# A delta-rule inverse packed as two diagonal blocks of 64, each block on its own quarter of TensorE

## The chip, the cores and the metric

The kernel runs on one core of one Trainium2 chip. The metric is the time of one execution on the device in microseconds (us). TensorE (PE) multiplies matrices, VectorE (DVE) and ScalarE (ACT) do elementwise work, SyncE (SP) issues the weight transfers. The four run from separate instruction streams and meet at semaphores.

## The reference, cut to what matters

Two model blocks run one after the other on 512 tokens. The first has two layers, and each of them holds a gated delta rule with 4 heads of 128. In each chunk of tokens the rule solves a unit lower triangular system:

```
a = jnp.where(strict, jnp.einsum('bhnik,bhnjk->bhnij', k_beta, k) * rel, 0.0)
eye = jnp.broadcast_to(jnp.eye(C, dtype=jnp.float32), a.shape)
rhs = jnp.concatenate([v * beta[..., None], k_beta * jnp.exp(decay)[..., None]], axis=-1)
sol = lax.linalg.triangular_solve(eye + a, rhs, left_side=True, lower=True, unit_diagonal=True)
```

The kernel uses chunks of 128 tokens, so it needs the inverse of `eye + a` for 4 chunks x 4 heads in each of the 2 layers. All of it is in fp32.

## The kernel before, in words

`gdn_pe`, `gdn_act` and `gdn_dve` hold the delta rule of one layer, one function for each engine's own stream. The four chunks are n = 0 to 3 (`TT` = 4). A tile 128x512 holds the four heads (`GH` = 4) of one chunk side by side, 128 columns each. `at_mat` is the transposed matrix a. `xt_inv` is the transposed inverse X^T as it grows, and `x_inv` is X.

The inverse is built by doubling. At level 0 the 2x2 diagonal blocks are inverted, by a mask (`level0`) and a subtraction from the identity. For each later level s (1 to 6) the blocks of size 2^s are joined in pairs:

1. DVE masks `at_mat` to the blocks of that level, into `tmp` (L1727, in `level`).
2. PE multiplies that by X (`level`, L1430), ACT copies the product out of PSUM into `yv` (L1596).
3. PE multiplies the product into X^T (`update`, L1443), DVE subtracts the result from X^T (L1754).
4. PE turns the new X^T into X by a transposing matmul (`turn`, L1417), ACT copies it out (L1586, in `turned`).

Level 6 joins the two blocks of 64. It uses only the corners that matter, with 64x64 matmuls (L1427, L1440), ACT copies of 64x256 (L1594) and DVE subtractions of 64x256 (L1754 in its short form). The turn before it is a 64x64 one as well (L1414, L1584).

The order on every engine is written out by hand. PE does the four updates of a level with the turns of the earlier chunks between them, then the four products of the next level with the last turn behind the first of them. PE waits in program order. PSUM has 8 banks that `claim` hands out in turn, and a bank is claimed again only when its reader has freed it.

Ahead of the levels stands a stretch in which the four chunks' rows, grams and scaled copies are made (L737, L1392, L1396, L1401 on PE, L1572, L1578, L1559 and L1563 on ACT, L1703 and L1712 on DVE). The first turns and the level-1 products are mixed into it. DVE's work of one chunk there is `products`: `at_mat` (L1712), `level0` (L1718), the first mask (L1727) and the subtraction from the identity (L1722). Behind the levels comes the recurrence over the chunks. It begins with L1489, which waits for the finished X^T, and pieces of the output projection (L648 to L650) are mixed in.

Between the levels DVE also does two 128x512 products of the attention matrix and the queries (`queries`, L1738 and L1741), at the start of levels 2 to 5. ACT applies Silu to one gate tile (`gate_act`, L1189) behind levels 1 to 4.

Every fp32 matmul shows in the trace as two records of a weight load and a matmul. A transposing one shows as one record of each. Other lines that the prediction uses: L832 and L868 are scores and values of the attention stages, where two heads of 64 take either two halves of the array's rows (L832, each head with a PSUM bank of its own) or two halves of its columns (L868, both heads in one bank). L591 to L593 are the big weight products.

Of the kernel before, what the change touches and what calls it, by code (L numbers as in the profile page):

```python
# [13 lines left out]
P = 128  # L14
D = 1024
KC = D // P
S = 512
# [184 lines left out]
def const_columns():  # L202
    c = Columns()
    for name in ("ident", "ones", "upto", "neg_future", "rope1", "rope2", "head_ones"):
        c.add(name, P)
    for s in range(7):
        c.add(f"level{s}", P)
    c.add("inv_freq", 1)
    c.add("eps", 1)
    c.add("eps_q", 1)  # L210
    c.add("zero", 1)
    return c


def constants():
# [25 lines left out]
    for s in range(7):  # L241
        put(f"level{s}", ((i >> s) % 2 == 1) & ((j >> s) == (i >> s) - 1))
# [122 lines left out]
def build(nc, dram, out, book):  # L365
# [18 lines left out]
    with ctx:  # L384
# [27 lines left out]
        with ExitStack() as a2:  # L412
            x_inv = sb(a2, "x_inv", [P, TT, S])
# [934 lines left out]
        UPPER, LOWER = slice(0, HALF), slice(HALF, P)  # L1348

# [57 lines left out]
        def gdn_pe(pe, l):  # L1407

            def turn(s, n):
                pe.wait_ge(*when("xt", l, s, n))  # L1410
                b = claim(pe, "xtr", l, s, n)
                for h in range(GH):
                    if s == 5:
                        mm = pe.transpose(head(b, h)[UPPER, 0:HALF], head(xt_inv[:, n, :], h)[UPPER, 0:HALF],  # L1414
                                          ident[UPPER, 0:HALF])
                    else:
                        mm = pe.transpose(head(b, h), head(xt_inv[:, n, :], h), ident)  # L1417
                mm.then_inc(*filled("xtr", l, s, n))

            def level(s, n):  # L1420
                if s < 6:
                    pe.wait_ge(*when("level", l, s, n))
                pe.wait_ge(*when("x", l, s - 1, n))
                b = claim(pe, "y", l, s, n)
                for h in range(GH):
                    if s == 6:
                        mm = pe.matmul(head(b, h)[LOWER, 0:HALF], head(at_mat[:, n, :], h)[UPPER, HALF:P],  # L1427
                                       head(x_inv[:, n, :], h)[UPPER, 0:HALF], start=True, stop=True)
                    else:
                        mm = pe.matmul(head(b, h), head(tmp[:, 4 + n, :], h), head(x_inv[:, n, :], h),  # L1430
                                       start=True, stop=True)
                mm.then_inc(*filled("y", l, s, n))

            def update(s, n):
                pe.wait_ge(*when("y_in", l, s, n))
                b = claim(pe, "pxt", l, s, n)
                for h in range(GH):
                    y = head(yv[:, n, :], h)
                    if s == 6:
                        mm = pe.matmul(b[UPPER, HALF * h:HALF * h + HALF], y[LOWER, 0:HALF],  # L1440
                                       head(xt_inv[:, n, :], h)[LOWER, HALF:P], start=True, stop=True)
                    else:
                        mm = pe.matmul(head(b, h), y, head(xt_inv[:, n, :], h), start=True, stop=True)  # L1443
                mm.then_inc(*filled("pxt", l, s, n))

            for n in range(1, TT):
                gdn_rows_pe(pe, l, n)
                gdn_grams_pe(pe, l, n)
                if n >= 2:
                    turn(0, n - 2)  # L1450
                if n >= 3:
                    level(1, n - 3)
            for n in range(TT - 2, TT):
                turn(0, n)
# [110 lines left out]
        def gdn_act(act, l):  # L1565
# [15 lines left out]
            def turned(s, n):  # L1581
                b = bank(act, "xtr", l, s, n)
                if s == 5:
                    op = act.activation(corner(x_inv[:, n, :], UPPER, 0), corner(b[:, :], UPPER, 0), ACT.Copy)  # L1584
                else:
                    op = act.activation(x_inv[:, n, :], b[:, :], ACT.Copy)  # L1586
                op.then_inc(*freed("xtr", l, s, n, also=("x", l, s, n)))

            def level(s, n):
# [5 lines left out]
                else:  # L1595
                    op = act.activation(yv[:, n, :], b[:, :], ACT.Copy)  # L1596
                op.then_inc(*freed("y", l, s, n, also=("y_in", l, s, n)))

            for n in range(TT):
                products(n)  # L1600
                scaled("kt", k_dec, KD, "kdec", n)
                if n >= 2:
                    turned(0, n - 2)
# [7 lines left out]
            for n in range(TT - 2, TT):  # L1611
                turned(0, n)
                level(1, n - 1)
            level(1, TT - 1)
            for s in range(1, 6):
                for n in range(1, TT):
                    turned(s, n - 1)
                level(s + 1, 0)
                turned(s, TT - 1)
                for n in range(1, TT):  # L1620
# [76 lines left out]
        def gdn_dve(dve, l):  # L1697
# [10 lines left out]
            def products(n):  # L1708
# [8 lines left out]
                xt3 = xt_inv[:, n, :].rearrange("p (h n) -> p h n", h=GH)  # L1717
                dve.tensor_tensor(xt3, at_mat[:, n, :].rearrange("p (h n) -> p h n", h=GH),  # L1718
# [1582 lines left out]
```

## Time and profile before

| what | value |
|---|---|
| median of 3 executions | 2566.98 us (2565.72 to 2568.05) |
| profiled execution, its own time | 2569.73 us |
| span of the profiled execution, first to last instruction | 2567.9 us |
| mean granted TensorE clock | 0.991 of full |
| PE busy | 2487.4 us, 97% of the span |
| DVE busy | 1655.4 us, 64% |
| ACT busy | 1126.9 us, 44% |
| levels 1 to 5 of the inverse in layer 0, up to level 6's first update | 229.52 to 272.87 us |
| the same in layer 1 | 1115.03 to 1158.40 us |

Times in the profile count from the span's start. A row of a timeline gives the start, the length up to the last end in the row, the engine, the line and the number of instructions joined in it. The length of a row holds the tail of its last instruction, so the pace of a stream is read from one row's start to the next row's start.

### The profile page before, as it was taken

Reading aid. Unit: us, or ns where it says so; the run is one execution under the profiler, and the core shown is the slowest. Engines: PE = TensorE matmul, PEld = TensorE weight load, DVE = VectorE, ACT = ScalarE, POOL = GpSimd, SP = SyncE. Lnnn points to the kernel's source line nnn. Section 1 sums busy time; section 2 is a strip of 40 time slices with the busy share of each in tenths; the row PEclk is TensorE's granted clock in tenths of the full one; section 3 lists DMA queues with packets and bytes.
Section 4 is the critical chain, followed back from the end, with each engine's and each line's share of the span. In section 5 each row is a group of like instructions: output and inputs, shape, how many; then the busy total and the mean of one; then the engine's idle time right before and its main releaser. Section 6 shows DMA issues by size and latency. Waiting matters only on the chain.

```text
span 2567.9 us, 34478 instructions
## 1 busy us (share of the span) xinstructions
PE 2487.4 (97%) x13166; PEld 2012.4 (78%) x13166; DVE 1655.4 (64%) x3170; ACT 1126.9 (44%) x2089; POOL 0.2 (0%) x4
## 2 busy tenths in 40 slices
PE   8998999999999999999999999999999999999998
PEld 6878888778888778798977888887866666788666
DVE  6666575464447785665744644488586677599774
ACT  4336454443333243464544423333446667232573
POOL 0000000000000000000000000000000000000000
PEclk9999999999999999999999999999999999999999
DMA  4220043222237522201422232464110000132311
GB/s 166 90 74 17 27 139 99 65 83 93 96 99 237 164 83 86 75 1 50 157 65 75 82 97 93 145 223 160 58 42 18 17 17 21 62 89 66 87 48 50
DMA packets 74083, 219.37 MB, mean 85 GB/s; under 512 B 21312, under 2 KB 21568, under 8 KB 73152
## 3 DMA queue, kind: packets, MB, share of 16 engines
q1 hardware_dynamic: 48384, 176.29, 21.0%
q10 hardware_dynamic: 25536, 40.87, 5.1%
q8 instruction: 107, 1.75, 0.3%
q14 instruction: 56, 0.46, 0.1%
HBM read 215.03 MB, written 2.10 MB: 85 GB/s over the span
## 4 chain that ended last, share of the span: by engine, by line
PE 87%; DVE 7%; ACT 3%; issue 2%; ACTq 0%; DMA 0%; DVEq 0%
PE bank L591 21%; PE bank L592 20%; PE bank L593 20%; PE bank L832 4%; PE bank L868 4%; PE bank L842 3%; DVE w_lo L553 2%; PE bank L1443 1%; PE bank L1430 1%; PE bank L622 1%; PE bank L624 1%; PE bank L623 1%; ACT w_hi L546 1%; PE bank L648 1%; PE bank L650 1%
## 5 line engine op out<-in xcount | busy, mean ns | idle before, releaser
L546 ACT ACTIVATE w_hi<-w_raw 128x1024 fp32r<-128x1024 f32 x334 | 354.3, 1062 | 572.4 <-PE bank L593 523.5
L553 DVE TENSOR_TENSOR w_lo<-w_raw,w_hi 128x1024 fp32r<-128x1024 f32 x334 | 408.1, 1223 | 234.8 <-ACT w_hi L546 233.8
L591 PE MATMUL bank<-a_hi,w_hi 128*128 128x512 f32 x1344 | 539.3, 401 | 20.0 <-DVE w_lo L553 18.0
L593 PE MATMUL bank<-a_hi,w_lo 128*128 128x512 f32 x1344 | 525.7, 391 | 0.0
L592 PE MATMUL bank<-a_lo,w_hi 128*128 128x512 f32 x1344 | 525.2, 391 | 0.0
L591 PEld LDWEIGHTS bank<-a_hi,w_hi 128*128 128x128 f32 x1344 | 251.9, 187 | 82.6 <-issue 18.4
L593 PEld LDWEIGHTS bank<-a_hi,w_lo 128*128 128x128 f32 x1344 | 251.8, 187 | 55.6
L592 PEld LDWEIGHTS bank<-a_lo,w_hi 128*128 128x128 f32 x1344 | 252.3, 188 | 52.5 <-issue 1.0
L591 PE MATMUL bank<-b_hi,w_hi 128*128 128x512 f32 x440 | 182.9, 416 | 4.2 <-DVE w_lo L553 2.7
L592 PE MATMUL bank<-b_lo,w_hi 128*128 128x512 f32 x440 | 173.2, 394 | 0.0
L593 PE MATMUL bank<-b_hi,w_lo 128*128 128x512 f32 x440 | 172.8, 393 | 0.0
L591 PE MATMUL bank<-f_hi,w_hi 128*128 128x512 f32 x352 | 137.0, 389 | 0.0
L593 PE MATMUL bank<-f_hi,w_lo 128*128 128x512 f32 x352 | 136.9, 389 | 0.0
L592 PE MATMUL bank<-f_lo,w_hi 128*128 128x512 f32 x352 | 136.9, 389 | 0.0
L3025 DVE CUSTOM_DVE_ANT_0 mod_part<-mod_raw,mod_cond,par 128x1024 f32<-128x1024 f32 x96 | 118.6, 1281 | 0.0
L591 PEld LDWEIGHTS bank<-b_hi,w_hi 128*128 128x128 f32 x440 | 82.9, 188 | 35.1 <-issue 28.3
L2960 DVE TENSOR_TENSOR tmp<-bank,rstd 128x512 f32<-128x512 f32 x44 | 30.4, 690 | 112.1 <-PE bank L593 112.1
L593 PEld LDWEIGHTS bank<-b_hi,w_lo 128*128 128x128 f32 x440 | 82.9, 188 | 19.0
L2420 DVE SCALAR_TENSOR_TENSOR c_y<-c_u,par,c_y 128x512 f32<-128x512 f32 x120 | 90.2, 751 | 3.7
L591 PE MATMUL bank<-m_hi,w_hi 128*128 128x256 f32 (+1 forms) x296 | 88.8, 300 | 0.8 <-DVE w_lo L553 0.8
L592 PEld LDWEIGHTS bank<-b_lo,w_hi 128*128 128x128 f32 x440 | 83.3, 189 | 7.7 <-issue 1.0
L593 PE MATMUL bank<-m_hi,w_lo 128*128 128x256 f32 (+1 forms) x296 | 88.0, 297 | 0.0
(444 smaller groups left out, 4453.3 us busy)
## 6 DMA issues: line engine op xcount, KB each, us to landing
w_raw<-w_tiles SPq DMA_DIRECT2D x334, 512.0 KB, 3.5
mod_raw<-mod_tiles ACTq DMA_DIRECT2D x48, 512.0 KB, 4.2
d_bias<-rpb_rows ACTq DMA_DIRECT2D x16, 224.0 KB, 4.3
hT<-xT ACTq DMA_DIRECT2D x8, 256.0 KB, 6.0
m_in<-memT ACTq DMA_DIRECT2D x2, 1024.0 KB, 4.8
mod_cond<-cond_rows ACTq DMA_DIRECT2D x2, 1024.0 KB, 5.9
out<-hT ACTq DMA_DIRECT2D x8, 256.0 KB, 2.2
ctx_sq<-ctxT ACTq DMA_DIRECT2D x1, 1024.0 KB, 7.7
```

The source lines that it names most:

```text
L546: act.activation(w_hi[:, t % SPLIT, :], w_raw[:, t % RAW, :], ACT.Copy).then_inc(sem("w_rounded"), 1)
L553: dve.tensor_tensor(w_lo[:, t % SPLIT, :], w_raw[:, t % RAW, :], w_hi[:, t % SPLIT, :].bitcast(f32), ALU.subtract).then_inc(sem("w_split"), 1)
L591: pe.matmul(o, wh, chunk(hi, k, n), start=k == 0, stop=False)
L592: pe.matmul(o, wh, chunk(lo, k, n), start=False, stop=False)
L593: mm = pe.matmul(o, wl, chunk(hi, k, n), start=False, stop=k == kc - 1)
L622: pe.matmul(outs[j][:, :n], wh, hi[:, k, :n], start=k == 0, stop=False)
L832: mm = pe.matmul(b[:, :nk], q, k, start=j == 0, stop=j == len(mms) - 1)
L842: mm = pe.transpose(b[:, P * j:P * j + P], s[:, u % s.shape[1], c:c + P], ident)
L868: mm = pe.matmul(b[rows * lane:rows * lane + rows, lo - base:hi - base], v, pt(lane, kt, kt + 1, lo - base, hi - base)[:, 0, :], start=n = ...
L2420: op = dve.scalar_tensor_tensor(out=c_y[:, c, :], in0=c_u[:, c, j:j + S], scalar=G("dw_w", CT * c + j), in1=c_y[:, c, :], op0=ALU.mult, op ...
L2960: dve.tensor_tensor(tmp[:, r + 2, :], b[:, :], rstd[:, :], ALU.mult)\
L3025: dve.tensor_tensor_reduce(mod_part[:, w, :], mod_raw[:, c % MOD_RAW, :], mod_cond[:, w, :], 1.0, G(f"mod_b{l}", c), ALU.mult, ALU.add, mo ...
```

## The change

The inverses up to level 5 are kept as two diagonal blocks of 64, since nothing outside these blocks is touched before level 6. The upper block lies on partitions 0 to 63 and the lower one on partitions 64 to 127, so a chunk's four heads take 256 columns in place of 512. X and X^T then fit into one tile, `xx_inv`: X in columns 0 to 255, X^T in 256 to 511.

- Each 128x128 matmul of levels 1 to 5 becomes two of 64x64, one on the upper rows and columns of the array (first in `QUADS`) and one on the lower.
- The turns of levels 1 to 5 go. In their place `update` makes both products, the change of X and the change of X^T, and DVE subtracts both from `xx_inv` in one instruction.
- The turn after level 0 stays, as an ordinary matmul with `ident_half` in place of a transposing one.
- The masks are 64 wide. DVE copies the diagonal blocks of `at_mat` next to each other first (two copies of 64x256 for each chunk), and each mask product covers 128x256.
- DVE does the mask product of a level ahead of the subtraction instead of behind it.
- At level 5 DVE writes the new X^T into the corners of `xt_inv`, in two instructions, beside one for X. `xt_inv` gets a zero corner from four memsets, and level 6 writes its corner by a product with -1 in place of a subtraction.

```
+            def turn(n):
+                pe.wait_ge(*when("xt", l, 0, n))
+                b = claim(pe, "xtr", l, n)
                 for h in range(GH):
+                    for q in QUADS:
+                        mm = pe.matmul(half(b, 0, h)[q], half(xx_inv[:, n, :], 1, h)[q], C("ident_half")[q, :],
+                                       start=True, stop=True, skip_group_check=True)
...
             def level(s, n):
-                pe.wait_ge(*when("x", l, s - 1, n))
+                pe.wait_ge(*(when("x", l, n) if s == 1 else when("xt", l, s - 1, n)))
...
-                        mm = pe.matmul(head(b, h), head(tmp[:, 4 + n, :], h), head(x_inv[:, n, :], h),
-                                       start=True, stop=True)
+                        for q in QUADS:
+                            mm = pe.matmul(half(b, 0, h)[q], half(tmp[:, 4 + n, :], 0, h)[q],
+                                           half(xx_inv[:, n, :], 0, h)[q],
+                                           start=True, stop=True, skip_group_check=True)
...
             def update(s, n):
-                        mm = pe.matmul(head(b, h), y, head(xt_inv[:, n, :], h), start=True, stop=True)
+                        for q in QUADS[:1] if s == 5 else QUADS:
+                            pe.matmul(half(b, 0, h)[q], half(xx_inv[:, n, :], 1, h)[q], half(yv[:, n, :], 0, h)[q],
+                                      start=True, stop=True, skip_group_check=True)
+                        for q in QUADS:
+                            mm = pe.matmul(half(b, 1, h)[q], half(yv[:, n, :], 0, h)[q],
+                                           half(xx_inv[:, n, :], 1, h)[q],
+                                           start=True, stop=True, skip_group_check=True)
...
             for s in range(1, 7):
                 for n in range(TT):
                     update(s, n)
-                    if s < 6 and n:
-                        turn(s, n - 1)
                 if s < 6:
-                    level(s + 1, 0)
-                    turn(s, TT - 1)
-                    for n in range(1, TT):
+                    for n in range(TT):
                         level(s + 1, n)
...
+                for q, at in zip(QUADS, (0, HALF)):
+                    op = dve.tensor_copy(by_half(halves(tmp[q, 4 + n, :], 1)), corner(at_mat[:, n, :], q, at))
+                op.then_inc(*done("blocks", l, n))
+                dve.wait_ge(*when("blocks", l, n))
+                xt3 = by_half(halves(xx_inv[:, n, :], 1))
+                dve.tensor_tensor(xt3, blocks_of(n), over_halves(C("level0")), ALU.mult)\
+                   .then_inc(*done("level0", l, n))
...
+            for n in range(TT):
+                dve.memset(corner(xt_inv[:, n, :], LOWER, 0), 0.0)
...
                 for n in range(TT):
-                    b = bank(dve, "pxt", l, s, n)
-                        x, change = xt_inv[:, n, :], b[:, :]
-                    dve.tensor_tensor(x, x, change, ALU.subtract)\
                     if s < 5:
                         level(s + 1, n)
+                    b = bank(dve, "pxt", l, s, n)
+                    if s < 5:
+                        op = dve.tensor_tensor(xx_inv[:, n, :], xx_inv[:, n, :], b[:, :], ALU.subtract)
+                    elif s == 5:
+                        x = halves(xx_inv[UPPER, n, :], 0)
+                        dve.tensor_tensor(x, x, halves(b[UPPER, :], 0), ALU.subtract)
+                        for q, at in zip(QUADS, (0, HALF)):
+                            op = dve.tensor_tensor(corner(xt_inv[:, n, :], q, at),
+                                                   by_half(halves(xx_inv[q, n, :], 1)),
+                                                   by_half(halves(b[q, :], 1)), ALU.subtract)
```

## Rows read from the trace of the kernel before

**Rows 1.** The page: busy time, share of the span and count of each engine.

```profile
PE 2487.4 (97%) x13166; PEld 2012.4 (78%) x13166; DVE 1655.4 (64%) x3170; ACT 1126.9 (44%) x2089; POOL 0.2 (0%) x4
```

**Rows 2.** Stretches: start:end, length, busy (count) PE, PEld, DVE, ACT, POOL, clock, DMA.

```profile
229.52:238.52 9.00, 9.00 (x83) 8.93 (x82) 6.15 (x10) 4.61 (x8) 0.00 (x0) 1.00 0.01 2
...
265.52:272.87 7.35, 7.35 (x80) 6.56 (x78) 2.75 (x4) 3.46 (x9) 0.00 (x0) 1.00 0.01 2
...
1115.03:1158.40 43.37, 43.37 (x401) 42.27 (x400) 27.37 (x44) 24.94 (x44) 0.00 (x0) 1.00 0.01 1
...
1094.00:1115.14 21.14, 17.40 (x112) 17.11 (x113) 14.64 (x39) 16.81 (x50) 0.00 (x0) 0.76 0.01 1
```

**Rows 3.** The chain that ended last, level 1 of layer 0: start, length, what.

```profile
232.12 0.89 PE bank L1443 x8
233.01 0.44 PE bank L1417 x4
...
234.78 0.89 PE bank L1430 x8
```

**Rows 4.** The timeline from 220 us: idle time and its releaser in brackets.

```profile
220.16 1.13 DVE L1703 SCALAR_TENSOR_TENSOR rel_t<-bank,col,con 128x128 f32<-128x128 f32 x4 [0.85 <-ACT dec L1559]
...
227.27 0.66 PE L1417 MATMUL bank<-con,xt_inv 128*128 128x128 f32 x4 [1.14 <-DVE xt_inv L1722]
...
227.96 0.60 ACT L1586 ACTIVATE x_inv<-bank 128x512 f32<-128x512 f32 x1 [0.52 <-PE bank L1417]
...
229.62 1.95 PE L1443 MATMUL bank<-xt_inv,yv 128*128 128x128 f32 x16
...
230.72 0.69 DVE L1754 TENSOR_TENSOR xt_inv<-xt_inv,bank 128x512 f32<-128x512 f32 x1 [3.51 <-PE bank L1443]
231.32 0.68 DVE L1727 TENSOR_TENSOR tmp<-at_mat,con 128x512 f32<-128x512 f32 x1
```

**Rows 5.** The timeline of PE in layer 1, ahead of the levels.

```profile
1095.77 1.97 PE L1401 MATMUL bank<-con,g_qkv 128*128 128x128 f32 x8 [2.94 <-DVE at_mat L1712]
```

**Rows 6.** The timeline of PE around level 6.

```profile
269.28 1.16 PE L1443 MATMUL bank<-xt_inv,yv 128*128 128x128 f32 x8
270.37 0.41 PE L1414 MATMUL bank<-con,xt_inv 64*64 64x64 f32 x4
270.71 0.68 PE L1427 MATMUL bank<-x_inv,at_mat 64*64 64x64 f32 x8
...
272.87 0.27 PE L1440 MATMUL bank<-xt_inv,yv 64*64 64x64 f32 x1
```

**Rows 7.** The timeline of all engines where level 6's update begins.

```profile
272.93 0.22 PE L1427 MATMUL bank<-x_inv,at_mat 64*64 64x64 f32 x1
...
272.98 0.22 PE L1440 MATMUL bank<-xt_inv,yv 64*64 64x64 f32 x1
...
273.04 0.22 PE L1427 MATMUL bank<-x_inv,at_mat 64*64 64x64 f32 x1
273.10 1.85 PE L1440 MATMUL bank<-xt_inv,yv 64*64 64x64 f32 x29
...
274.88 1.16 PE L1489 MATMUL bank<-v_beta,xt_inv 128*128 128x128 f32 x8
```

**Rows 8.** Groups of matmuls, shapes apart: count, busy us, mean ns, idle before.

```profile
L868 PE MATMUL bank<-e_pt,e_vt 128*64 128x256 f32 x384 | 46.7, 385 | 5.4 <-ACT e_pt L992 5.4
...
L832 PE MATMUL bank<-xk,xq 128*128 128x256 f32 x128 | 33.0, 381 | 1.3 <-DVE xq L2882 1.3
L868 PE MATMUL bank<-x_pt,xvt 128*128 128x512 f32 x64 | 28.8, 592 | 0.0
...
L832 PE MATMUL bank<-e_kd,e_q 64*128 64x512 f32 x64 | 21.3, 641 | 0.0
```

**Rows 9.** Groups by shape, 229 to 275 us, DVE and ACT.

```profile
L1754 DVE TENSOR_TENSOR xt_inv<-xt_inv,bank 64x256 f32<-64x256 f32 x4 | 1.7, 414 | 2.6 <-PE bank L1440 2.4
...
L1594 ACT ACTIVATE yv<-bank 64x256 f32<-64x256 f32 x4 | 1.5, 380 | 0.9 <-PE bank L1427 0.5 <-PE bank L1440 0.4
```

More of the change, by code:

```diff
@@ L205, in const_columns @@
         c.add(name, P)
-    for s in range(7):
-        c.add(f"level{s}", P)
+    c.add("ident_half", P // 2)
+    for s in range(6):
+        c.add(f"level{s}", P // 2)
     c.add("inv_freq", 1)
@@ L240, in constants @@
     put("head_ones", (j // 64) == (i // 64))
-    for s in range(7):
-        put(f"level{s}", ((i >> s) % 2 == 1) & ((j >> s) == (i >> s) - 1))
+    jh, ih = j % (P // 2), i[:, :P // 2]
+    put("ident_half", jh == ih)
+    for s in range(6):
+        put(f"level{s}", ((ih >> s) % 2 == 1) & ((jh >> s) == (ih >> s) - 1))
     freq = np.float32(500000.0) ** (-np.arange(0, 2 * ROPE_HALF, 2, dtype=np.float32) / (2 * ROPE_HALF))
@@ L1348, in build, with half, halves, by_half @@
         UPPER, LOWER = slice(0, HALF), slice(HALF, P)
+        QUADS = (UPPER, LOWER)
+        def half(ap, w, h):
+            return ap[:, (GH * w + h) * HALF:(GH * w + h) * HALF + HALF]
+        def halves(ap, w):
+            return ap[:, GH * HALF * w:GH * HALF * (w + 1)]
+        def by_half(ap):
+            return ap.rearrange("p (h n) -> p h n", h=GH)
+        def over_halves(ap):
+            return ap[:, None, :].broadcast_to([P, GH, HALF])
         def l2_sums_pe(pe, l):
@@ L1449, in gdn_pe @@
                 if n >= 2:
-                    turn(0, n - 2)
+                    turn(n - 2)
                 if n >= 3:
@@ L1453, in gdn_pe @@
             for n in range(TT - 2, TT):
-                turn(0, n)
+                turn(n)
                 level(1, n - 1)
@@ L1579, in scaled, with turned @@
                 op.then_inc(*freed(name, l, n, also=(event, l, n)))
[L1581 to L1587, printed above, removed]
+            def turned(n):
+                b = bank(act, "xtr", l, n)
+                act.activation(halves(xx_inv[:, n, :], 0), halves(b, 0), ACT.Copy)\
+                   .then_inc(*freed("xtr", l, n, also=("x", l, n)))
             def level(s, n):
@@ L1595, in level @@
                 else:
-                    op = act.activation(yv[:, n, :], b[:, :], ACT.Copy)
+                    op = act.activation(halves(yv[:, n, :], 0), halves(b, 0), ACT.Copy)
                 op.then_inc(*freed("y", l, s, n, also=("y_in", l, s, n)))
@@ L1602, in gdn_act @@
                 if n >= 2:
-                    turned(0, n - 2)
+                    turned(n - 2)
                 if n + 1 < TT:
@@ L1611, in gdn_act @@
             for n in range(TT - 2, TT):
-                turned(0, n)
+                turned(n)
                 level(1, n - 1)
@@ L1735, in gdn_dve @@
                     products(n - 1)
+            for n in range(TT):
+                dve.memset(corner(xt_inv[:, n, :], LOWER, 0), 0.0)
             def queries(n):
```

43 lines of the change are left out of this document (13 added, 30 removed).

## The prediction

> **What bounds the kernel now.** I read the page first. TensorE (PE) is busy for 2487.4 us, 97% of the span [rows 1], so work taken off PE counts if nothing takes its place. Then I asked for stretches around the delta rule. One level there, from the first update of level 1 to that of level 2, takes 9.00 us. PE is busy for all 9.00, DVE for 6.15, ACT for 4.61 [rows 2]; levels 2 to 4 read the same within 0.01. Level 5 with the products of level 6 takes 7.35. The reader should see that DVE and ACT have room and PE has none.
>
> The chain of waits shows the same by pieces: an update of one chunk is 8 records in 0.89 us, a turn 4 records in 0.44, a product 8 records in 0.89 [rows 3]. Four chunks give 4 x (0.89 + 0.44 + 0.89) = 8.88, and 0.12 is left for waits. Layer 1 has the same 43.37 us over its levels [rows 2] (layer 0: 4 x 9.00 + 7.35 = 43.35).
>
> **What a 64x64 record costs.** Level 6 has such matmuls already, one tile at a time. L1414, 4 records, goes from 270.37 to 270.71, with a change of tile shape at its front: 0.085 us each. L1440's last 29 records start at 273.10 and L1489, which follows, starts at 274.88: 1.78 / 29 = 0.061, with the drain [rows 6, 7]. Eight L1427 at 270.71 last 0.68, and a single such record 0.22 [rows 6, 7], so seven steps take 0.46: 0.066 with the first one's start-up. I take 0.058, which is the step inside the alternating rows below, and keep 0.061 for the range. A 128x128 record steps by 0.89 / 8 = 0.111.
>
> Now the count. Before, a chunk and level has 20 records. After, the product has 4 heads x 2 tiles x 2 = 16, the update 4 x 4 x 2 = 32, together 48. One after the other these would take 48 x 0.058 = 2.78 us, against 2.22 before. So all depends on whether the two tiles run at the same time.
>
> **What the trace shows of two tiles at once.** Three places.
> - Where level 6's update begins, L1427 (upper rows, lower columns) and L1440 (lower rows, upper columns) alternate: L1440 at 272.87, L1427 at 272.93, L1440 at 272.98, L1427 at 273.04, L1440 at 273.10 [rows 6, 7]. Each tile steps by 0.055 to 0.06 on its own and does not slow the other. L1440 stands behind all of L1427 in the program, so it even ran past it.
> - Two halves of the columns, same bank: L868 with 64 columns takes 46.7 / 384 = 0.122 us for 256 moving columns, a full-array record of that length 33.0 / 128 = 0.258 [rows 8].
> - Two halves of the rows, a bank each: L832 with 64 rows takes 21.3 / 64 = 0.333 for 512, a full one 28.8 / 64 = 0.450 [rows 8]. This includes tails of groups with one pair only; it is weaker, but the same sign.
>
> What no row shows is the exact case: diagonal tiles for a long time, both writing one bank in different partitions.
>
> **The sum, layer by layer.**
> 1. Levels 1 to 4. With both tiles at work a chunk costs 24 x 0.058 = 1.39 us, a level 5.57. I add 0.09 for waits as before: 5.66. Removed against added: 9.00 - 5.66 = 3.34 a level, 13.4 for four.
> 2. Is DVE then the bound? Its two instructions of a chunk started 0.60 apart at 512 columns [rows 4]. A 64x256 subtraction took 0.414 against 0.69 at 512 [rows 4, 9], so the new 128x256 mask costs about 0.60 - 0.27 = 0.33. A chunk is 0.93, four are 3.7, with the two attention products (1.2) 4.9: under 5.66. The tightest wait is for chunk 3. Its update ends 3.71 + 0.2 after the level's start, DVE is through at about 4.6 to 4.7, and PE wants it at 3.71 + 3 x 0.46 = 5.1. If DVE's instructions did not overlap (0.69 + 0.41 a chunk), the level would be 5.8: 0.15 x 8 = 1.2 us in all, kept for the range. The mask product now stands ahead of the subtraction; it waits only for the earlier product, done long before.
> 3. ACT: the turned copies (0.60) go, the rest shrink from 0.60 to 0.38 [rows 4, 9]. A product of chunk 0 is out 0.46 + 0.2 + 0.38 = 1.0 us after its start, and the update that needs it starts 1.9 after. The gates' Silu lies in the free time. Each level claims 8 banks in place of 12, so a bank comes round after a level, long freed.
> 4. Level 5. The update's upper tile has 16 records for a chunk: 0.93, four 3.71. DVE needs three 64-row instructions a chunk, 3 x 0.34 = 1.0, and starts 1.14 in, so it ends at 5.3. Level 6's product of chunk 3 waits for that and ends near 5.8, where level 6's update begins. Before: 7.35 [rows 2], with pauses, for each switch between 128 and 64 wide tiles lengthened an update from 0.89 to 1.09 [rows 3, 6]. Gain 1.5.
> 5. Level 6's update and what follows keep their shape; the product with -1 costs what the subtraction did (0.41). Nothing.
> 6. Ahead of level 1. DVE's work for a chunk loses three 512-wide instructions and gets five 256-wide ones and one more wait: 3 x 0.60 against 5 x 0.33 + 0.1, even. DVE waits there for ACT (0.85 at 220.16) [rows 4], and ACT's turned copy ahead of it shrinks by 0.22. At the end, turn 3 starts at 227.27, its copy takes 0.60 at 227.96, and the first update starts at 229.62 after two products of 0.89 [rows 4]. After: turn to 227.95, copy to 228.35, one product of 0.46 behind it, update at 228.85. Together 0.9. The four memsets lie in DVE's idle 3.51 us before its first subtraction [rows 4].
> 7. The rest of the kernel hangs on PE's progress, so it moves up as it is. The masks' load shrinks; no PE wait hangs on it.
>
> Sum: 13.4 + 1.5 + 0.9 = 15.8 a layer, 31.6 for two. The profiled execution took 2569.73 (span 2567.9, 1.8 around it), 2.7 above the median, so it would be 2538.1, and the median 2566.98 - 31.6 = 2535.4 us.
>
> **Rivals.**
> - **The tiles take turns** (slower). If two tiles that write one bank cannot run together, a chunk costs 2.78, a level 11.2, 2.2 more than now, 8.9 a layer over four levels; level 5 comes out even (4 x 24 x 0.058 + 1.9 = 7.4). 2567.0 + 17.8 = 2585. It decides from 0.093 us for a pair of records on (8.91 / 96). For it: no row has row halves in one bank. Against it: L868's column halves share one and run together, and the partitions here are as separate as those. Chance 0.12. A page speaks for this rival: the Trainium skill, "TensorEngine Tiling (Array Packing)", "Gotcha 1: PSUM Pressure", says that different row tiles cannot access the same PSUM bank at the same time. By that rule the time would be this rival's 2585; no run here shows it yet, since L832's row tiles had a bank each.
> - **Instructions come too slowly.** Twice the records must be issued in each microsecond as in any long stretch before. The 6-record stretch at 272.87 may have lived on a queue filled ahead. If a pair takes 0.087, half way between both cases, a level is 8.4 (gain 0.6), level 5 gains 0.8, the front 0.4: 3.6 a layer, 2560. Chance 0.14. The Trainium skill, the same page, "Instruction Overhead", has about 60 cycles for a matmul however few its columns and advises against tiling an already small dimension; two of them at 2.4 GHz would be 0.05, under the 0.058 used here.
> - **The clock falls to 1.2 GHz** (slower), since each tile pair fills half the array. The levels then cost twice 0.058 for a pair, as in the first rival: 2585 or a little above. For it: in layer 1 the mean granted clock ahead of the levels was 0.76, in a stretch where PE had sat idle for 2.94 us [rows 2, 5]. Against it: the stretch with level 6's single 64x64 tiles ran at 1.00 [rows 2], and PE will not be idle. Chance 0.06.
> - A shift of where the low clock falls ahead of the levels: layer 1 needed 19.3 us from its first gap (1095.77) to level 1 (1115.03). A second such stretch in layer 0, or none in layer 1, is worth about 2.5 us either way. It changes the range, not the case.
>
> **How the numbers follow.** Both tiles together: 0.68, 2535.4, own range 2529 to 2545 (the clock 2.5 either way, 0.061 for 0.058 costs 8 x 0.29 = 2.3, DVE 1.2, the front and level 5 worth 1 a layer more or less). To leave out no more than 2 in 10 the range must take in the second rival to 2562: 2528 to 2562. About what this kernel's times can tell from no change is 0.2%, 5.1 us. Faster: 0.68 and most of the 0.14, 0.80. The same: 0.04. Slower: 0.16, both slow rivals less a little.
>
> **What would show it.** A level 5.6 to 5.8 us long with PE busy throughout, 192 matmul records in it, rows of upper and lower tile in pairs; DVE's idle time before a subtraction small; no record of L1417. Wrong, if a level takes 8.4 or 11.2 us, if the clock reads 0.5 inside the levels, or if PE waits for `xx_inv` in each level: then DVE is the bound and item 2 failed. Level 5 is wrong if level 6's update starts later than 6.5 us after level 5's first.

## The result

The changed kernel took 2534.8 us (median of 4 runs, 2533.35 to 2537.24), the kernel before on the same chip 2566.8 (4 runs). The ratio is 0.9877, with a 95% interval of 0.9862 to 0.9892: faster by 32 us. The forecast was 2535.4. One execution of the kernel before, in the first series of the experiments below, took 10193.89 us for a reason that nothing here shows, and no ratio counts it.

The page of the changed kernel, against [rows 1]: TensorE has 1,152 records more and is busy for 35.5 us less.

```profile
PE 2451.9 (97%) x14318; PEld 1978.0 (78%) x14318; DVE 1650.8 (65%) x3210; ACT 1093.9 (43%) x2049; POOL 0.2 (0%) x4
```

Stretches of the changed kernel, in the columns of [rows 2]. The first two are level 1 and level 3 of layer 0; then come level 1 and level 2 of layer 1, and the last is from level 5's first update to the first product of the recurrence (here L1507, before L1489).

```profile
231.41:237.01 5.60, 5.60 (x199) 5.60 (x197) 4.43 (x9) 1.32 (x4) 0.00 (x0) 1.00 0.01 3
242.83:249.16 6.33, 5.98 (x198) 5.79 (x196) 5.34 (x12) 2.09 (x6) 0.00 (x0) 1.00 0.01 3
...
1100.69:1106.29 5.60, 5.60 (x199) 5.60 (x197) 4.43 (x9) 1.32 (x4) 0.00 (x0) 1.00 0.01 3
1106.29:1111.89 5.60, 5.60 (x199) 5.60 (x197) 5.03 (x11) 3.45 (x7) 0.00 (x0) 1.00 0.02 6
1123.09:1131.41 8.32, 7.63 (x168) 7.29 (x164) 6.12 (x16) 3.74 (x10) 0.00 (x0) 1.00 0.01 2
```

The reader is to see 5.60 where [rows 2] have 9.00, at a granted clock of 1.00, with PE busy for all of it. The 199 records are the level's 192 and some that overlap the edges. The second row is longer and not busy throughout; I come back to it.

How both tiles work side by side is seen in the timeline of PE where level 1 of layer 1 begins. L1460 is X's change, L1463 that of X^T:

```profile
1100.69 0.31 PE L1460 MATMUL bank<-yv,xx_inv 64*64 64x64 f32 x4
1100.81 0.31 PE L1463 MATMUL bank<-xx_inv,yv 64*64 64x64 f32 x4
1100.93 0.31 PE L1460 MATMUL bank<-yv,xx_inv 64*64 64x64 f32 x4
1101.04 0.31 PE L1463 MATMUL bank<-xx_inv,yv 64*64 64x64 f32 x4
```

Four records start every 0.117 us, two of the upper and two of the lower tile (by the order of the loops): a pair each 0.058. All of a chunk's update write one bank. 96 pairs x 0.058 = 5.6 us.

**Where the 32 us come from.** By the starts of the stretches in both traces:

| stretch | layer 0 before, after | layer 1 before, after |
|---|---|---|
| last gap of PE ahead of the levels to level 1's first update | 16.82, 15.67 | 19.37, 16.63 |
| levels 1 to 4 | 36.00, 23.63 | 36.01, 22.40 |
| level 5's first update to the recurrence's first product | 9.26, 8.26 | 9.25, 8.32 |
| gain | 1.2 + 12.4 + 1.0 | 2.7 + 13.6 + 0.9 |

That is 31.8 of the 33.7 us by which the spans differ (2567.9 and 2534.2). The other 1.9 lie outside, and the low stretches of the clock account for most of them. The changed kernel reached layer 0's last gap 2.9 later (215.74 against 212.80). Its first products stepped by 0.43 us until 15.65, those of the kernel before only until 12.70, and by 0.23 from there. So it worked 2.95 us longer at the slow step, which did there what takes 1.6 at the fast one: 1.4 lost. And it had a stretch at half clock from 50.1 to 53.5, where the kernel before had none, for another 1.6. What follows layer 1's levels was 4.7 us shorter: the work there is the same (7,182 records of PE in both), but the kernel before spent 27.2 us of it at half clock and the changed one 17.0. By the same steps the 10.2 us between them are worth 4.7, if PE is the bound throughout. These three prices are estimates.

Ahead of the levels layer 0 had no low clock in either kernel, and gained 1.15. So of layer 1's 2.7 some 1.6, most of it, is the clock: the kernel before had two stretches at half clock there, the changed one only one.

```profile
1095.00:1101.80 6.80, 6.03 (x29) 6.04 (x30) 5.05 (x15) 4.79 (x15) 0.00 (x0) 0.50 0.00 1
1108.65:1112.06 3.41, 3.41 (x19) 3.41 (x18) 3.38 (x9) 2.30 (x8) 0.00 (x0) 0.50 0.03 5
```

These are of the kernel before. Of the changed one, with 3.4 us at half clock from 1084.3 on:

```profile
1084.06:1087.70 3.64, 3.64 (x18) 3.64 (x19) 1.91 (x6) 2.70 (x10) 0.00 (x0) 0.53 0.02 5
```

### The profile page after: what moved, and what is told of

Same layout as the page of the kernel before. It is cut to its first block, busy times and chain, and to the rows that moved or that the text cites. A ratio compares the mean times of both kernels' runs of the same rounds, so it can differ in the third digit from the quotient of the medians.

```text
span 2534.2 us, 36742 instructions
## 1 busy us (share of the span) xinstructions
PE 2451.9 (97%) x14318; PEld 1978.0 (78%) x14318; DVE 1650.8 (65%) x3210; ACT 1093.9 (43%) x2049; POOL 0.2 (0%) x4
## 4 chain that ended last, share of the span: by engine, by line
PE 86%; DVE 8%; ACT 4%; issue 2%; ACTq 0%; DMA 0%; DVEq 0%
PE bank L594 21%; PE bank L595 20%; PE bank L596 20%; PE bank L835 4%; PE bank L871 4%; PE bank L845 3%; DVE w_lo L556 2%; PE bank L625 1%; PE bank L627 1%; PE bank L626 1%; ACT w_hi L549 1%; PE bank L651 1%; PE bank L653 1%; PE bank L652 1%; PE bank L1463 1%
## 5 line engine op out<-in xcount | busy, mean ns | idle before, releaser
L596 PEld LDWEIGHTS bank<-b_hi,w_lo 128*128 128x128 f32 x440 | 82.6, 188 | 18.9
L595 PE MATMUL bank<-m_lo,w_hi 128*128 128x256 f32 (+1 forms) x296 | 88.0, 297 | 0.0
```

The costliest lines, as they stand in the source:

```text
L595: pe.matmul(o, wh, chunk(lo, k, n), start=False, stop=False)
L596: mm = pe.matmul(o, wl, chunk(hi, k, n), start=False, stop=k == kc - 1)
```

## The experiments

Eight kernels ran: the first four beside one series of the kernel before (2568.3 us median), the next three beside another (2566.8), the last beside a third (2566.3). Times are medians.

### Order of the tiles

Is it the alternation of upper and lower tile that makes both work? Here a chunk's products of the upper tile are all issued before those of the lower tile, in the turn, the product and the update. The records are the same ones.

```diff
-                for h in range(GH):
-                    for q in QUADS:
+                for q in QUADS:
+                    for h in range(GH):
```

> The same matmuls on PE in another order: in each group of levels 0 to 5 all of the upper tile's records first, then all of the lower tile's (8 and 8 in a product, 16 and 16 in an update). Theory: the gain hangs on both tiles at work at once, and a tile holds only a few records ahead (three were seen), so the tiles overlap only at the ends of groups. A level of layer 1 (5.60 us in the changed kernel) becomes 8 to 10 us, the time some 2555 to 2575 us. Rival 1, it is the smaller tile or the missing turns that gain, not the overlap: a level stays at 5.6 and the time at 2535. Rival 2, no overlap at all unless records alternate: 4 x 48 x 0.058 = 11.1 us a level, 5.5 x 8 = 44 us, about 2580. If PE looks past more than eight records the level also stays near 5.6; then the rows tell it from rival 1, since upper and lower records still start together.

Measured: 2555.87 us, 0.9954 of before (0.994 to 0.9969). A level takes 8.33 us in both layers. One stretch, layer 1's level that starts at 1111.27, and the timeline of PE at its start:

```profile
1111.27:1119.60 8.33, 8.33 (x198) 8.33 (x195) 4.94 (x10) 1.24 (x4) 0.00 (x0) 1.00 0.01 2
```

```profile
1111.27 0.27 PE L1461 MATMUL bank<-yv,xx_inv 64*64 64x64 f32 x1
1111.32 0.22 PE L1446 MATMUL bank<-xx_inv,tmp 64*64 64x64 f32 x1
1111.38 0.22 PE L1461 MATMUL bank<-yv,xx_inv 64*64 64x64 f32 x1
1111.38 0.22 PE L1446 MATMUL bank<-xx_inv,tmp 64*64 64x64 f32 x1
...
1111.44 0.22 PE L1446 MATMUL bank<-xx_inv,tmp 64*64 64x64 f32 x1
```

The update's first upper record (L1461) starts ahead of the last three lower records of the product (L1446), as L1440 did ahead of three L1427 in the kernel before ([rows 7] have the first of these three and the last; I give the other under the account of the prediction). Behind these rows only the upper tile works (L1461 and L1464 are both its own), record by record at 0.058, until the lower tile's come. The numbers close: 192 records one by one are 11.14 us; a level has 16 changes from one tile to the other, each with three steps side by side, so 11.14 - 16 x 3 x 0.058 = 8.36 against 8.33. Counted in this level's trace, at each of the 16 changes exactly three steps have a second record beside them, and at no other. So the gain of the tiles hangs on the order of issue. The six records in alternation that the prediction rested on [rows 6, 7] were this look ahead of three, not yet proof of a steady state; the change has that state because it issues the tiles in turn.

### Packed, with the turns kept

The tiles without the other half of the change: X is again the turned X^T (a turn of 8 pairs of records a chunk and level, copied by ACT), in place of the 8 pairs of X's change.

```diff
-                pe.wait_ge(*(when("x", l, n) if s == 1 else when("xt", l, s - 1, n)))
+                pe.wait_ge(*when("x", l, s - 1, n))
...
-                        for q in QUADS[:1] if s == 5 else QUADS:
-                            pe.matmul(half(b, 0, h)[q], half(xx_inv[:, n, :], 1, h)[q], half(yv[:, n, :], 0, h)[q],
...
                     update(s, n)
+                    if s < 6 and n:
+                        turn(s, n - 1)
```

> Packed in blocks of 64 as in the changed kernel, but X comes from a turn at levels 1 to 5, as before: the update makes only the change of X transposed, an identity matmul turns it and ACT copies it out. PE has as many 64x64 records a level (16 + 16 + 16 for a chunk). Theory: the turnless update gives no PE time, it only takes away waits; a level is 5.6 to 6.1 us, the time 2535 to 2540. Rival: the turn's chain (DVE, PE, ACT, PE) no longer fits into a level this short, as each step covers less work: a level of 6.5 to 7.5, the time 2543 to 2552.

Measured: 2538.62 us, ratio 0.9885 (0.9868 to 0.9903). A level takes 5.87 us in layer 1. Level 2 of that layer as a stretch, and PE's timeline at its start (L1464 is X^T's change, L1435 the turn, which begins anew behind each update):

```profile
1106.93:1112.80 5.87, 5.81 (x199) 5.68 (x196) 4.14 (x10) 4.82 (x11) 0.00 (x0) 1.00 0.02 6
```

```profile
1106.93 1.10 PE L1464 MATMUL bank<-xx_inv,yv 64*64 64x64 f32 x32
1108.08 0.68 PE L1435 MATMUL bank<-con,xx_inv 64*64 64x64 f32 x16
```

The count of records is the same as without turns (14318 on both pages). The extra 0.27 us a level is a wait of some 0.3 between the two rows: the first turn stands behind DVE's subtraction. Over eight levels this is 2.2 us, and ACT is busy for 4.82 in place of the changed kernel's 3.45. The packing carries nearly all of the gain; what the turnless update adds, 3.8 us by the medians and 2 by the ratios, is about as large as this kernel's times can tell: the changed kernel itself gave 2534.8 in one series and 2538.1 in another, below. The 2.2 us are read from the traces.

### DVE's order

The changed kernel puts the mask product of the next level ahead of the subtraction; here it stands behind, as before.

```diff
-                    if s < 5:
-                        level(s + 1, n)
                     b = bank(dve, "pxt", l, s, n)
...
                     op.then_inc(*freed("pxt", l, s, n, also=("xt", l, s, n)))
+                    if s < 5:
+                        level(s + 1, n)
```

> Only DVE's order undone: the mask product of the next level stands behind the subtraction again. Theory: the order is worth nothing, since DVE has about half a microsecond to spare for chunk 3 and the mask fits in it; 5.60 us a level, time within 0.1% of the changed kernel (2533 to 2537). Rival: the mask of chunk 3 comes too late for its product, 0.1 to 0.33 us a level, 1 to 3 us in all.

Measured: 2536.15 us, ratio 0.9876 (0.9855 to 0.9898), levels of 5.60 us in both layers. No difference. DVE has the room: in the changed kernel's timeline of DVE at level 1 of layer 1 a chunk takes 0.93, as forecast, and a level has idle time at its start. Below, L1771 subtracts, L1745 masks.

```profile
1101.86 0.69 DVE L1771 TENSOR_TENSOR xx_inv<-xx_inv,bank 128x512 f32<-128x512 f32 x1 [1.28 <-PE bank L1463]
1102.46 0.42 DVE L1745 TENSOR_TENSOR tmp<-tmp,con 128x256 f32<-128x256 f32 x1
1102.80 0.68 DVE L1771 TENSOR_TENSOR xx_inv<-xx_inv,bank 128x512 f32<-128x512 f32 x1
```

### Level 6's product waits for X alone

At level 5 DVE has three instructions a chunk: X's upper block (L1774), then the two blocks of X^T (L1776, twice). Level 6's product reads X alone, but waits for the last of the three. Here it waits for the first.

```diff
-                pe.wait_ge(*(when("x", l, n) if s == 1 else when("xt", l, s - 1, n)))
+                pe.wait_ge(*(when("x", l, n) if s == 1 else when("x_last", l, n) if s == 6 else when("xt", l, s - 1, n)))
...
-                        dve.tensor_tensor(x, x, halves(b[UPPER, :], 0), ALU.subtract)
+                        dve.tensor_tensor(x, x, halves(b[UPPER, :], 0), ALU.subtract).then_inc(*done("x_last", l, n))
```

> One event more: at level 5 DVE says that X is ready behind its first instruction of a chunk, and level 6's product waits for that in place of all three. Theory: in the changed kernel level 5 lasts 8.32 us up to the first product of the recurrence, 0.5 more than forecast, because DVE needs 1.22 us for a chunk and each product waits for the last of its three instructions. Then this run shortens it by 0.4 to 0.8 us a layer, about 1 us in all (2533 to 2535, not to be told from the changed kernel by time, but by the profile). Rival: the update of level 6 waits for the last corner anyway and the stretch stays at 8.2 to 8.3.

Measured: 2534.03 us, ratio 0.9865 (0.9848 to 0.9882). From level 5's first update to the recurrence's first product it takes 7.55 us in layer 0 and 7.54 in layer 1. The changed kernel's timeline there shows what was removed; PE first, then DVE:

```profile
1127.90 0.68 PE L1442 MATMUL bank<-xx_inv,at_mat 64*64 64x64 f32 x8 [0.16 <-DVE xt_inv L1776]
1129.12 0.50 PE L1442 MATMUL bank<-xx_inv,at_mat 64*64 64x64 f32 x5 [0.54 <-DVE xt_inv L1776]
1129.40 0.27 PE L1456 MATMUL bank<-xt_inv,yv 64*64 64x64 f32 x1
```

```profile
1124.24 0.41 DVE L1774 TENSOR_TENSOR xx_inv<-xx_inv,bank 64x256 f32<-64x256 f32 x1 [0.89 <-PE bank L1463]
1124.58 0.84 DVE L1776 TENSOR_TENSOR xt_inv<-xx_inv,bank 64x256 f32<-64x256 f32 x2
1125.45 0.41 DVE L1774 TENSOR_TENSOR xx_inv<-xx_inv,bank 64x256 f32<-64x256 f32 x1
```

DVE needs 1.21 us a chunk (1124.24 to 1125.45) and PE stands for its last instruction twice. With X alone awaited, 8.32 becomes 7.54, for 0.8 a layer. The trace shows it in both layers; the time of 2534.0 against 2534.8 can't.

### Neither packed nor turned

The other half of the change by itself: matrices of 128x128 as before, but X's change is computed in the update and subtracted by DVE, and the turns of levels 1 to 5 go.

```diff
             def update(s, n):
                 pe.wait_ge(*when("y_in", l, s, n))
+                if s < 6:
+                    b2 = claim(pe, "px", l, s, n)
+                    for h in range(GH):
...
+                            mm = pe.matmul(head(b2, h), head(xt_inv[:, n, :], h), y, start=True, stop=True)
...
-                    if s < 6 and n:
-                        turn(s, n - 1)
```

> The kernel before (matrices of 128x128) with the turns taken away and nothing packed: the update of levels 1 to 5 computes X's change as well as that of X^T, and DVE subtracts both, so a chunk has 24 products of 128x128 as before (8 for the level product, 8 for X's change, 8 for X^T's). My theory: what pays in the change is the packing; records of 128x128 step every 0.111 us with or without turns. Before, a level had 24 of them a chunk too, but 8 were turns that came in between; 4 x 24 x 0.111 = 10.7 us bounds a level where before took 9.00 (turns of 0.056 us a step). So a level gets longer by 1.7 us, 4 levels and 2 layers 13 us, level 5 about nothing: 2580 us, ratio 1.005. Rival: before was bound by its chain of turn and copy, and the turnless update alone carries a good part of the gain: a level below 9.0 us, and a time of 2550 or less.

Measured: 2585.73 us, ratio 1.0073 (1.0056 to 1.0089): slower. A level takes 10.72 in both layers, and from level 5 to the recurrence 10.47:

```profile
1134.45:1145.17 10.72, 10.72 (x99) 10.72 (x98) 8.58 (x14) 4.30 (x6) 0.00 (x0) 1.00 0.01 2
1166.70:1177.17 10.47, 10.47 (x130) 9.65 (x129) 5.35 (x11) 3.76 (x9) 0.00 (x0) 1.00 0.00 0
```

The level is what 96 x 0.111 gives (10.7). My expectation's reason was wrong beside that: [rows 3] have a turn as 4 records of 0.111 each, not as 8 of 0.056. I had put level 5 down at nothing; it costs 10.47 - 9.25 = 1.2 a layer. PE's timeline there shows X's change as 8 records in 0.61 us where the turn had 4 in 0.34 [rows 6]:

```profile
1166.70 0.67 PE L1442 MATMUL bank<-yv,xt_inv 64*64 64x64 f32 x8
1167.31 1.16 PE L1453 MATMUL bank<-xt_inv,yv 128*128 128x128 f32 x8
```

The sum is 8 x 1.72 + 2 x 1.2 = 16.2; the medians differ by 18.9, the spans by 14.7 (2582.6 against 2567.9). So a turnless update on full matrices loses: a turn is 4 records in 0.44 us [rows 3], X's change 8 in 0.89. In tiles both cost 8 pairs a chunk, 0.47, about what the old turn did, and the update with X's change is free of the wait.

### The changed kernel again

Unaltered, to see whether the pauses of layer 0 belong to its work.

> The changed kernel once more, unaltered. Time 2534 to 2537 us. The question is its layer 0: in the first profile its levels took 5.60, 5.82, 6.33 and 5.88 us, with five pauses of TensorE of 0.1 to 0.57 us that each began 2.1 to 2.5 us behind a transfer of 16 KB on the queue that brings instructions, while layer 1 ran 5.60 each time. If the pauses are late instructions, which depends on when a transfer falls, they come at other places or not at all in this profile, and the sum for layer 0's four levels lies between 22.4 and 24.5 us. If they belong to the work of layer 0 (a wait for data), they stand at the same distance from the start of level 1.

Measured: 2538.10 us (median of 4, 2537.21 to 2542.58), ratio 0.989 (0.9875 to 0.9904). The profiled execution was the longest of these, 2542.58. It stands 3.3 us above the first measuring of the same kernel, though both series put it at 0.988 to 0.989 of before. Stretches: levels 2, 3 and 4 of layer 0, then all four levels of layer 1.

```profile
237.24:242.84 5.60, 5.60 (x200) 5.60 (x197) 5.03 (x11) 3.45 (x7) 0.00 (x0) 1.00 0.02 6
242.84:248.73 5.89, 5.89 (x199) 5.79 (x196) 5.32 (x12) 2.07 (x6) 0.00 (x0) 1.00 0.01 3
248.73:254.61 5.88, 5.82 (x200) 5.74 (x197) 4.90 (x11) 2.02 (x6) 0.00 (x0) 1.00 0.02 6
...
1104.26:1126.66 22.40, 22.40 (x775) 22.40 (x772) 19.52 (x39) 8.88 (x20) 0.00 (x0) 1.00 0.02 4
```

Layer 0's four levels took 22.97 us, against 23.63 in the first profile and 22.40 where nothing pauses. Two of the five pauses are gone, that of level 2 and the longest, in level 3. The three others are back, and at the same places. Counted in PE's records from level 1's first update, the changed kernel paused behind records 301, 426, 552, 554 and 677, and this run behind 552, 554 and 677. The last of them in both, the changed kernel first:

```profile
252.08 0.55 PE L1463 MATMUL bank<-xx_inv,yv 64*64 64x64 f32 x3
```

```profile
251.65 0.55 PE L1463 MATMUL bank<-xx_inv,yv 64*64 64x64 f32 x3
```

From level 1's first update that is 20.67 and 20.01 us, and 19.84 and 19.85 without the pauses ahead of it. My expectation had two answers: other places or none, or the same distance each time. The record gives neither whole. Where a pause can fall is fixed by the program. Whether it falls there is not, so it isn't a wait for data that the work brings with it.

### X's subtractions pulled ahead

On top of the wait for X alone, DVE subtracts X of chunk n+1 ahead of the blocks of X^T of chunk n.

```diff
+                        held.append((n, b))
+                        for m, c in held[:-1] if n < TT - 1 else held:
                             for q, at in zip(QUADS, (0, HALF)):
-                                op = dve.tensor_tensor(corner(xt_inv[:, n, :], q, at),
+                                op = dve.tensor_tensor(corner(xt_inv[:, m, :], q, at),
...
+                        held = held[-1:]
```

> The changed kernel with level 6's product waiting for X alone, as in the run that did this alone, and at level 5 DVE subtracting X of chunk n+1 ahead of the two blocks of X^T of chunk n. In that earlier run the last chunk's product still stood 0.27 us for the fourth subtraction of X, which had 3 x 1.22 us of DVE ahead of it; here it has 1.66 + 0.8 = 2.9 us ahead, so this wait goes, and from level 5's update to the first product of the recurrence 7.54 us become 7.1 to 7.3. DVE's sum is unaltered, and its last subtraction ends at the same time, so that if the recurrence waits for it, nothing is gained. Time: 2 x (0.78 + 0 to 0.4) us below the changed kernel, 2532 to 2533 us, a ratio of 0.9985 to 0.9995 to it, hardly more than can be told.

Measured: 2536.13 us (2535.05 to 2537.38), ratio 0.9879 (0.9864 to 0.9893), 2.0 us below the unaltered kernel on the same chip, which is within what can be told. The stretch that it was made for did not shrink: 7.72 us in layer 0 and 7.64 in layer 1, against 7.55 and 7.54. My expectation of 7.1 to 7.3 was wrong. DVE's timeline, layer 1 (L1775 is X, L1779 the blocks of X^T):

```profile
1123.47 0.41 DVE L1775 TENSOR_TENSOR xx_inv<-xx_inv,bank 64x256 f32<-64x256 f32 x1 [0.89 <-PE bank L1463]
1124.41 0.41 DVE L1775 TENSOR_TENSOR xx_inv<-xx_inv,bank 64x256 f32<-64x256 f32 x1 [0.52 <-PE bank L1463]
1124.74 0.84 DVE L1779 TENSOR_TENSOR xt_inv<-xx_inv,bank 64x256 f32<-64x256 f32 x2
...
1127.17 1.73 DVE L1779 TENSOR_TENSOR xt_inv<-xx_inv,bank 64x256 f32<-64x256 f32 x4
1128.93 1.56 DVE L1786 TENSOR_SCALAR xt_inv<-bank 64x256 f32<-64x256 f32 x4
```

The second X has to wait for chunk 1's update, and DVE stands idle for 0.52 us that it had spent on chunk 0's blocks. The last X starts 3.36 us after the first (1126.83), 0.28 earlier than with no reordering (3.64), but DVE's last block ends at 1128.90, 5.43 us after the first X and not 4.82, which is later by the idle time and a little. ACT's copy of the last product waits for that block, since in the program that copy waits for the chunk's X^T, which the update behind it reads. The timelines of ACT and PE, layer 1:

```profile
1128.93 0.38 ACT L1609 ACTIVATE yv<-bank 64x256 f32<-64x256 f32 x1 [0.50 <-DVE xt_inv L1779]
```

```profile
1129.36 0.68 PE L1456 MATMUL bank<-xt_inv,yv 64*64 64x64 f32 x8 [0.17 <-ACT yv L1609]
```

So PE no longer waited for X, but for the copy behind DVE's last block: one wait was traded for another. (The 2.9 us in my expectation were added up wrongly too; three X and two pairs of blocks are 3 x 0.34 + 2 x 0.87 = 2.8, and 0.52 idle makes 3.3.)

### Only the last X pulled ahead

That reading can be tested. If the idle time in DVE was the fault, the order X0, blocks, X1, blocks, X2, X3, blocks of both has none of it.

```diff
                         held.append((n, b))
-                        for m, c in held[:-1] if n < TT - 1 else held:
+                        for m, c in () if n == TT - 2 else held:
...
-                        held = held[-1:]
+                        held = held if n == TT - 2 else []
```

> As the run before, but only the last chunk's X is pulled ahead: X0, its blocks, X1, its blocks, X2, X3, then the blocks of both. In the run before DVE stood 0.52 us for chunk 1's update; here X3 can start no sooner than chunk 3's update is through, 3 x 0.93 = 2.8 us after X0, and DVE reaches it after 2 x 1.21 + 0.34 = 2.8 us, so there is no idle time and DVE's last block ends as early as with no reordering. X3 then starts 0.8 us earlier than the 3.64 of the run with the wait on X alone, TensorE doesn't stand for it (0.27 there), and ACT's last copy isn't late as in the run before (where TensorE stood 0.17 for it). If I have now read the chain rightly, from level 5's first update to the recurrence's first product it takes 7.2 to 7.35 us, against 7.54 and 7.64. Rival: something else that I haven't seen bounds this stretch at 7.5, and it stays there. Time: 0.998 to 1.0 of the changed kernel, about 2533 to 2536 us on its scale; the time won't tell it, the stretch will.

Measured: 2534.09 us (2530.05 to 2544.8), ratio 0.9884 (0.9865 to 0.9902). The stretch took 7.21 us in layer 0 and 7.35 in layer 1 (there with one pause of 0.14 inside an update):

```profile
1118.04:1125.39 7.35, 7.35 (x167) 7.21 (x162) 6.10 (x16) 3.38 (x9) 0.00 (x0) 1.00 0.01 2
251.12:258.33 7.21, 7.21 (x169) 7.14 (x165) 6.15 (x16) 3.45 (x9) 0.00 (x0) 1.00 0.01 3
```

PE is busy for all of it, so it is the bound there now. Against the changed kernel's 8.26 and 8.32 this is 1.0 us a layer, the best version by the trace. By its time it can't be told from the changed kernel.

## Why the prediction was right, step by step

**The two tiles at once, one bank** (0.68 against 0.12 for taking turns): right. The pair costs 0.058, as taken, in a steady state of 96 pairs a level. The first rival's 11.2 us a level did not come. By the rule of the Trainium skill, "TensorEngine Tiling (Array Packing)", "Gotcha 1: PSUM Pressure", it should have; the trace here disagrees for diagonal tiles, whose partitions in the bank differ (5.60 us for 192 records, all into the bank of their chunk). The six records that the prediction took for both tiles at work don't show it as listed: there each tile steps by 0.11 us (L1440 at 272.87, 272.98, 273.10), which a single stream in turn would give too. The whole view has one L1427 more between them and another start at 273.04, and with these each tile steps by 0.055 to 0.06 from 272.98 on:

```profile
272.99 0.22 PE L1427 MATMUL bank<-x_inv,at_mat 64*64 64x64 f32 x1
273.04 0.22 PE L1440 MATMUL bank<-xt_inv,yv 64*64 64x64 f32 x1
```

The order test adds a condition that the prediction didn't have: the tiles must alternate in the program, or only three steps at each change overlap.

**Instructions fast enough** (rival at 0.14): nearly. In the first profile layer 1 ran at full pace in all levels, and layer 0 lost 1.2 us. The rival had 8.4 us for a level, 2.8 above the 5.60, or 11 a layer. Something like it seems to exist, as argued below, at about a tenth of that price: 0 to 1.2 us a layer.

**Item 1, levels 1 to 4:** 13.4 forecast, 13.6 in layer 1, 12.4 in layer 0. The 0.09 us a level for waits were not needed: 5.60, not 5.66.

**Item 2, DVE:** 0.93 a chunk, measured 0.94 (1101.86 to 1102.80). It was to be through with chunk 3 at 4.6 to 4.7 after the level's start; the last subtraction starts at 1104.67 and takes 0.68, so it ends 4.66 after. Right, and the order of mask and subtraction makes no difference.

**Item 3, ACT:** right; a 128x256 copy takes 0.38, and PE never waits for one inside a level.

**Item 4, level 5:** 1.5 forecast, 1.0 and 0.9 measured. About 0.1 of the forecast was a mark: the 7.35 begin 0.1 ahead of level 5's first update, from which the table above counts. The rest is DVE, and the step that failed is "3 x 0.34 = 1.0 per chunk". Only the first instruction has a step of 0.34; the pair behind it takes 0.84 and the next chunk starts after 1.21. DVE therefore ends 5.97 us after the level's start (1129.06), not 5.3, and level 6's update starts at 6.31, not 5.8 (still under the 6.5 that would have been the sign of a wrong level 5). The bound on this item had been 1 a layer more or less, which held.

**Item 5, level 6's update:** unchanged, as taken.

**Item 6, ahead of level 1:** 0.9 forecast, 1.15 in layer 0. From the last turn to the first update 2.35 us became 1.69, for 0.66 where 0.77 was forecast; ahead of that turn it was 0.49 where 0.13 was. Layer 1's 2.7 contains the clock, which the prediction had as plus or minus 2.5 in the range without a sign.

**The clock** did not fall in levels 1 to 5: 1.00 in each row here, and no stretch at half clock between level 1's first update and level 6's in any of the kept traces. Behind them it can. In two of the traces it fell to half in layer 0 while level 6's update ran, from 260.7 us with the mask product behind and from 262.0 in the changed kernel's second profile, each time for 6.8 us. PE had stood for some 0.16 and for 0.54 us just ahead. The update of 2.00 us then took 3.51 and 2.68, the first of them here:

```profile
260.52:264.03 3.51, 3.51 (x40) 3.39 (x38) 1.25 (x3) 2.57 (x5) 0.00 (x0) 0.52 0.00 0
```

The same two waits stand in the changed kernel's layer 1 (1127.90 and 1129.12, above), where the clock stayed at 1.00, so they don't decide it alone.

The sum was 31.6 and the medians differ by 32.0. Part of that closeness is luck: the levels and level 5 together gave 27.9 against 29.8 forecast, and the front with its clock 3.9 against 1.8. And of the 33.7 us between the two profiled executions some 3 are the clock's and not the change's (1.6 + 4.7 - 3.0, an estimate from the prices above).

## What to carry to other kernels

If a PE-bound stretch multiplies block-diagonal matrices with halves of 64, put the two blocks on diagonal tiles and issue them in turn, matmul by matmul: here a level fell from 9.00 to 5.60 us, and with the same records grouped by tile only to 8.33. Price each half of a change by itself: the turnless update made the unpacked kernel 0.7% slower and the packed one hardly faster. Where several instructions end with one event, look which of them the reader needs; and before pulling one of them ahead, see whether its input is there yet.

## What the runs showed of the hardware beyond the forecast

**A look ahead of three.** With one tile's records grouped, the other tile started three records early at every change, and no more, in 16 changes a level (8.33 us measured, 8.36 by that count). No run here varied that number, so whether it depends on the length of the groups (8 and 16 records here) or the size of the tiles is open.

**Pauses that no wait explains.** In layer 0 of the changed kernel PE stops five times inside the levels, which makes them 1.2 us longer. The longest, in PE's timeline:

```profile
244.00 0.22 PE L1460 MATMUL bank<-yv,xx_inv 64*64 64x64 f32 x1
244.57 0.21 PE L1460 MATMUL bank<-yv,xx_inv 64*64 64x64 f32 x1 [0.35 <-issue]
```

It stops in the middle of an update, and no semaphore releases it. The DMA view of 240 to 250 us (40 slices of 0.25 us) has three packets in that time, all on the queue of kind "instruction", 16 KB each:

```profile
DMA  0000000300000000000000030000000000000030
...
q8 instruction: 3, 0.05, 2.4%
```

They lie at 241.8, 245.8 and 249.7. In five of the profiles I found 17 such pauses, of 0.1 to 0.6 us from one start to the next (five here, three in the repetition, two with the turns kept, two and five in the last two runs), and each starts 1.8 to 2.7 us after such a transfer. The runs with the mask product behind and with the wait for X alone have the same pace and as many transfers and no pause in levels 1 to 4 of either layer. Layer 1 has none in most profiles, but four in the last run, where level 3 took 6.26 us:

```profile
1105.93:1112.19 6.26, 5.89 (x200) 5.78 (x195) 5.69 (x12) 2.54 (x7) 0.00 (x0) 1.00 0.01 3
```

So they go with no layer, but they do go with a place in the program. In layer 0, where six profiles of five kernels have the same stream on PE, pauses stand behind records 301 (two profiles), 426 (one), 552 (three) and 677 (two), each with at most one short one right behind, and nowhere else in levels 1 to 4; in layer 1 of the last run behind 576 and 702 and, in level 5, behind 826. Both rows step by 124 to 126 records. With the weight loads that is about 250 instructions, and one transfer of 16 KB comes for about as many (six in the 768 records of a layer's four levels). Blocks of instructions of that size, each fetched as a whole, would put the pauses there. A level issues 384 instructions of PE (192 products, 192 weight loads) in 5.60 us where there were some 160 in 9.00, and the transfers come every 3.8 us in layer 1 in place of every 12 to 18. With the tiles grouped, at 8.33 us a level, they come every 5.5 us and nothing pauses. That PE runs out of instructions there is argued from this, not shown: the places fit, but no experiment changed the fetching alone, and most transfers are followed by no pause. The price was 0 to 1.2 us a layer, of 2535.
